# A four-layer trunk on one core: the program's head loads its vectors from another queue and re-orders its first steps

## The chip, the cores and the metric

The kernel runs on one core of one Trainium2 chip. The metric is the device time of one execution in microseconds (us), on the slowest core, which here is the only one.

## The reference

The reference puts 16 meta tokens ahead of 512 tokens of 1024 channels (528 tokens in all) and runs four layers. Each layer is a mixer and a gated feed-forward block, each added to the residual `h`. The mixers are pooling (layers 0 and 3), differential attention (layer 1) and a conformer convolution (layer 2). All is in fp32. Only the start of layer 0 matters here:

```python
h = jnp.concatenate([meta, x], axis=1)
y = rmsnorm(h, norm_mix_g[0])                   # over 1024 channels
# pool_mixer: per group of 256 channels, windows 2, 4, 8, 16
pooled = stack([trailing_mean(y_g, win) - y_g for y_g, win in groups])
mixed = einsum('blgc,gcd->blgd', pooled, pool_w[0]).reshape(B, L, 1024)
h = h + (mixed + pool_b[0]) * pool_scale[0]
h = h + swiglu_ffn(rmsnorm(h, norm_ffn_g[0]), ...)   # then layers 1 to 3
```

## The kernel before

Channels lie on the 128 partitions in 8 blocks, tokens along the free dimension. Every product of fp32 matrices is made of three rounded ones: each operand is split into a high half (`_hi`, a rounding copy on ScalarE) and a low half (`_lo`, a subtraction on VectorE), and TensorE adds hi\*hi, hi\*lo and lo\*hi. The program is written engine by engine; semaphores order the engines, and each engine runs its list in order.

The head of the program is all that the change touches. Before layer 0 can begin:

- SyncE (SP) issues six loads of `x` into `x_rows` (five tiles of tokens: 128, 128, 128, 127 and 32 rows; L639 to L643). It then waits until GpSimd has zeroed `vec_rows` (L779) and issues twelve loads of small vectors into `vec_rows`, 50 rows of 1024 floats (L649 to L654: norm gains, biases, convolution taps). Then come the four tiles of pool weights (`w_raw`, L659), the lambda vectors, and the bias table.
- TensorE runs 6 fill matmuls whose result nobody reads (`unread`, L1716), transposes the five tiles of `x_rows` (L1725), 6 more fills, waits for all twelve vector loads, transposes `vec_rows` (L1731), 15 fills, then begins the pool products `z` (L1039: 120 matmuls on `y` and the pool weights).
- VectorE copies each transposed tile into `h` (L3021), then the vectors into `vec` (L3027), which raises `vec_ready`.
- ScalarE sums the squares of the rows of each tile of x (L2199, the token sums), splits two pool weight tiles (L1802), waits for `vec_ready`, and makes the eight blocks `y_hi` (L1807) with two more weight halves between. It then rounds the band matrices (`bands`, L1856), the small matrices that take the trailing means.

After that VectorE turns the token sums into row factors (L2426 and the steps behind it, `tok_ready`), but only behind the low part of `bands` (L2478). ScalarE scales `z` by them into `z_hi` (L1874, five tiles, two `add_bias` steps L1862 between), VectorE makes `z_lo` (L2495), and TensorE multiplies z by the bands (`windows`, L1078 to L1087). The first of these waits for four tiles of `z_lo`. From there on TensorE works through windows, feed-forward and the later layers.

Of the kernel before, what the change touches and what calls it, by code (L numbers as in the profile page):

```python
# [31 lines left out]
ACT = mybir.ActivationFunctionType  # L32
ds = bass.ds

P = 128
# [5 lines left out]
NB = D // P  # L41
# [7 lines left out]
TAPS = 31  # L49
# [10 lines left out]
TILES = 5  # L60
# [293 lines left out]
class Semaphores:  # L354

    def __init__(self, sem):
# [5 lines left out]
        self.bias_in = sem("bias_in")  # L363
        self.gain_in = sem("gain_in")
        self.out_done = sem("out_done")
        self.vec_zeroed = sem("vec_zeroed")
        self.vec_ready = sem("vec_ready")
        self.consts_ready = sem("consts_ready")
        self.rel_ready = sem("rel_ready")
# [200 lines left out]
def trunk(nc, a, out):  # L570
    cols, first = plan()
    tiles = len(cols)
    ctx = ExitStack()
    with ctx:
# [62 lines left out]
        def _(sp):  # L637
# [3 lines left out]
            for i in range(1, TILES):  # L641
                t, n = TILE_STARTS[i] - META, LAST if i == TILES - 1 else P
                sp.dma_start(m.x_rows[0:n, i, :], a["x"][0, t:t + n, :]).then_inc(x_in[i], 16)  # L643
            sp.wait_ge(s.vec_zeroed, 1)
            for row, name in ((ROW_MIX, "norm_mix_g"), (ROW_FFN, "norm_ffn_g"), (ROW_POOL_B, "pool_b"),
                              (ROW_POOL_S, "pool_scale"), (ROW_DWB, "conv_dw_b"), (ROW_LNG, "conv_ln_g"),
                              (ROW_LNB, "conv_ln_b"), (ROW_CONV_OUT, "conv_b_out")):
                n = a[name].shape[0]
                sp.dma_start(m.vec_rows[row:row + n, :], a[name]).then_inc(s.vec_in, 16)  # L649
            sp.dma_start(m.vec_rows[ROW_CONV_IN:ROW_CONV_IN + 2, :],  # L650
                         a["conv_b_in"].rearrange("o (r n) -> (o r) n", r=2)).then_inc(s.vec_in, 16)
            for t, n in ((0, 16), (16, TAPS - 16)):
                sp.dma_start(m.vec_rows[ROW_DW + t:ROW_DW + t + n, :], a["conv_dw_w"][0, t:t + n, :]).then_inc(s.vec_in, 16)
            sp.dma_start(m.vec_rows[ROW_SUBLN:ROW_SUBLN + 1, 0:P], a["attn_subln_g"]).then_inc(s.vec_in, 16)  # L654

            def load(off, i, per, src, at_col, width):

                slot = off % SLOTS
# [117 lines left out]
        @block.gpsimd  # L776
        def _(pool):

            pool.memset(m.vec_rows[:, :], 0.0).then_inc(s.vec_zeroed, 1)  # L779
            pool.memset(m.tok_x[:, :], 1.0).then_inc(s.tok_cleared, 1)  # L780
            pool.memset(m.rms_eps, RMS_EPS)
            pool.memset(m.ln_eps, LN_EPS)
# [188 lines left out]
        def _(pe):  # L971
# [741 lines left out]
            def unread(n):  # L1713

                for _ in range(n):
                    pe.matmul(ps[:, 6, 0:P], m.ones[:, :], m.ones[:, :], start=True, stop=True)  # L1716
# [3 lines left out]
            for i, n in enumerate(TILE_ROWS):  # L1720
# [4 lines left out]
                    mm = pe.transpose(ps[:, 2 * (i % 3) + d // 4, (d % 4) * P:(d % 4) * P + n],  # L1725
                                      m.x_rows[0:n, i, d * P:(d + 1) * P], m.ident[0:n, 0:n])
                mm.then_inc(s.rows_turned, 1)
            unread(6)
            pe.wait_ge(s.vec_in, 16 * 12)
            for d in range(NB):  # L1730
                mm = pe.transpose(ps[:, 7, d * ROWS:(d + 1) * ROWS], m.vec_rows[:, d * P:(d + 1) * P],  # L1731
# [61 lines left out]
        def _(act):  # L1793
            def split_hi(t, i, per, n):

                if n == 0:
                    return
                slot = t % SLOTS
                act.wait_ge(raw_in[slot], (i * (per // SLOTS) + (t // SLOTS + 1 + pairs_done(first, t))) * 16)
                if t >= SLOTS:  # L1800
                    act.wait_ge(s.tile_used, i * per + (t - SLOTS + 1))
                act.activation(m.w_hi[:, slot, 0:n], m.w_raw[:, slot, 0:n], ACT.Copy).then_inc(s.hi_ready, 1)  # L1802

            def y_hi(d, hn, yn, row, t0, n):

                act.wait_ge(s.h_ready, d + (NB * hn + 1))
                act.activation(blk(m.y_hi, d, t0, n), blk(m.h, d, t0, n), ACT.Copy, scale=vec_col(row, d))\  # L1807
                   .then_inc(s.y_hi_ready, 1)
# [38 lines left out]
            def pool_layer(name, which, r, y_in, hn, yn, row):  # L1847
                tile0 = first[name]
                if name == "pool0":
                    act.wait_ge(s.vec_ready, 1)  # L1850
                    for d in range(NB):
                        y_hi(d, H_IN, Y_POOL0, ROW_MIX + 0, 0, TOK)
                        if d in (1, 3):
                            split_hi(tile0 + (3 + d) // 2, 0, 0, cols[tile0 + (3 + d) // 2])
                    act.wait_ge(s.band_built, 1)
                    act.activation(m.bands[:, :, 0:LOW0], m.bands_raw[:, :, :], ACT.Copy).then_inc(s.band_hi_ready, 1)  # L1856
                else:
                    act.wait_ge(s.token_sums, r + 1)
                act.wait_ge(s.vec_bias_ready, 1)
                def add_bias(d):  # L1860
                    act.wait_ge(s.y_ready, NB * y_in + d + 1)
                    act.activation(blk(m.h, d), blk(m.h, d), ACT.Identity, bias=m.pool_bs[:, which, d:d + 1])\  # L1862
                       .then_inc(s.h_biased, 1)
                if name == "pool0":
                    act.wait_ge(s.band_ready, 1)
                    act.dma_start(bands_dram, m.bands[:, :, :].bitcast(F32)).then_inc(s.bands_out, 16)
                act.wait_ge(s.tok_ready, which + 1)
                for i in range(TILES):
                    if i < TILES - 1:
                        act.wait_ge(s.z_done, (TILES - 1) * which + i + 1)  # L1870
                    else:
                        act.wait_ge(s.tile_used, tile0 + 4)
                    base, n = 2 * (i % 4), TILE_ROWS[i]
                    act.activation(m.z_hi[0:n, i, :].rearrange("p (b n) -> p b n", b=2), ps[0:n, base:base + 2, :],  # L1874
                                   ACT.Copy, scale=m.tok_r[0:n, i:i + 1]).then_inc(s.z_hi_ready, 1)
                    if i in (1, 2) and name == "pool0":
                        add_bias(i - 1)
                for c in (4, 5):
                    split_hi(tile0 + c, 0, 0, cols[tile0 + c])
                if name == "pool0":  # L1880
                    add_bias(2)
                for d in range(NB):
                    y_hi(d, hn, yn, row, 0, TOK)
                    act.activation(blk(m.x_square, d), blk(m.h, d), ACT.Square).then_inc(s.square_ready, 1)
                    if name == "pool0" and d + 3 < NB:
                        add_bias(d + 3)
                if name == "pool0":
                    act.wait_ge(s.rel_ready, 1)
                    act.dma_start(rel_once, m.rel[:, :]).then_inc(s.rel_once_out, 16)
# [303 lines left out]
                        split_hi(first["attn_out"] + NB + c, 0, 0, 512)  # L2193

            act.wait_ge(s.tok_cleared, 1)
            for i, n in enumerate(TILE_ROWS):
                act.wait_ge(x_in[i], 32 if i == 0 else 16)
                e = act.activation(m.row_squares[0:n, i, :], m.x_rows[0:n, i, :], ACT.Square,  # L2199
                                   accum_out=m.tok_x[0:n, i:i + 1])  # L2200
            e.then_inc(s.token_sums, 1)
            for t in range(2):
                split_hi(t, 0, 0, cols[t])
            pool_layer("pool0", 0, R_POOL0, Y_POOL0, H_POOL0, Y_FFN0, ROW_FFN + 0)
            act.wait_ge(s.lam_sums, 1)
            act.activation(m.lam_s[:, 2:4], m.lam_s[:, 0:2], ACT.Exp).then_inc(s.lam_exps, 1)
# [146 lines left out]
        def _(dve):  # L2353
            def split_lo(t, i, per, n):

                if n == 0:
                    return
                slot = t % SLOTS
                dve.wait_ge(s.hi_ready, i * per + (t + 1))
                dve.tensor_tensor(m.w_lo[:, slot, 0:n], m.w_raw[:, slot, 0:n],  # L2360
                                  m.w_hi[:, slot, 0:n].bitcast(F32), ALU.subtract).then_inc(s.lo_ready, 1)

            def y_lo(d, yn, row, t0, n):

                dve.wait_ge(s.y_hi_ready, d + (NB * yn + 1))
                dve.scalar_tensor_tensor(out=blk(m.y_lo, d, t0, n), in0=blk(m.h, d, t0, n), scalar=vec_col(row, d),
                                         in1=blk(m.y_hi, d, t0, n).bitcast(F32), op0=ALU.mult, op1=ALU.subtract)\
                   .then_inc(s.y_ready, 1)
# [89 lines left out]
            def pool_layer(name, which, r, yn, hn, row):  # L2458
# [9 lines left out]
                                             in1=blk(m.h, d), op0=ALU.mult, op1=ALU.add).then_inc(s.h_ready, 1)  # L2468

                if name == "pool0":  # L2470
                    for c in (0, 1):
                        split_lo(tile0 + c, 0, 0, cols[tile0 + c])
                    for d in range(NB):
                        y_lo(d, Y_POOL0, ROW_MIX + 0, 0, TOK)
                        if d in (1, 3):
                            split_lo(tile0 + (3 + d) // 2, 0, 0, cols[tile0 + (3 + d) // 2])
                    dve.wait_ge(s.band_hi_ready, 1)
                    dve.tensor_tensor(m.bands[:, :, LOW0:BANDS], m.bands_raw[:, :, FIRST0:FIRST0 + EDGE],  # L2478
                                      m.bands[:, :, FIRST0:FIRST0 + EDGE].bitcast(F32), ALU.subtract)\
                       .then_inc(s.band_ready, 1)  # L2480
# [544 lines left out]
            e.then_inc(s.h_ready, NB)  # L3025
            dve.wait_ge(s.rows_turned, TILES + 1)
            dve.tensor_copy(m.vec[:, :], ps[:, 7, 0:NB * ROWS]).then_inc(s.vec_ready, 1)  # L3027
            dve.drain()
            by_block = m.vec[:, :].rearrange("p (d r) -> p r d", d=NB)
            dve.tensor_tensor(m.pool_bs[:, :, :], by_block[:, ROW_POOL_B:ROW_POOL_B + 2, :],  # L3030
                              by_block[:, ROW_POOL_S:ROW_POOL_S + 2, :], ALU.mult).then_inc(s.vec_bias_ready, 1)
# [242 lines left out]
```

## Time and profile before

| | us |
|---|---|
| median of 3 runs | 1983.63 (1983.15 to 1984.39) |
| the profiled execution | 1983.36 |
| its span in the trace | 1981.6 |
| TensorE busy | 1965.5 (99%) |
| VectorE busy | 1569.5 (79%) |
| ScalarE busy | 933.8 (47%) |
| GpSimd busy | 208.6 (11%) |
| mean DMA rate | 99 GB/s |

Times in rows are microseconds from the span's start unless marked ns. PE is TensorE (PEld its weight loads), DVE VectorE, ACT ScalarE, POOL GpSimd, SP SyncE; a q behind an engine's name is its sequencer, where DMAs are issued. A busy TensorE is not always useful: fills count as busy too. An fp32 matmul on `ones` shows as two records, so 15 fills are 30 records.

### The profile page before, as it was taken

What the parts mean: (1) busy time and instruction counts of PE and PEld (TensorE: products, weight loads), DVE (VectorE), ACT (ScalarE), POOL (GpSimd) and SP (SyncE); (2) the same over time, 40 slices, a digit from 0 to 9 for tenths busy, and PEclk for the clock granted to TensorE, in tenths of its full rate; (3) what the DMA queues carried; (4) which work ended last, traced back from release to release, by engine and by line L of the source; (5) the groups of instructions that cost most, each with busy time, mean ns of one, the idle gap of its engine ahead of it and who ended that gap; (6) DMA issues with size and microseconds to landing.
All of it is one profiled execution on the core that took longest, in us unless ns stands there. A gap on an engine that the chain in (4) does not pass through costs nothing.

```text
span 1981.6 us, 39851 instructions
## 1 busy us (share of the span) xinstructions
PE 1965.5 (99%) x15718; PEld 1909.9 (96%) x15718; DVE 1569.5 (79%) x2171; ACT 933.8 (47%) x1484; POOL 208.6 (11%) x325
## 2 busy tenths in 40 slices
PE   9999999999999999999999999999999999999998
PEld 8999999999999999999999989999999998989997
DVE  6797788767788788877979997697778768977794
ACT  7443333346676534433447785343334454433343
POOL 5000000241111200000051212000000140000000
PEclk9999999999999999999999999999999999999999
DMA  5433342342111324233335762223243323323232
GB/s 171 140 86 106 86 127 81 92 129 64 54 57 52 96 86 128 67 103 93 94 113 130 163 139 64 86 86 107 85 126 85 114 70 107 112 80 104 86 107 96
DMA packets 305390, 196.82 MB, mean 99 GB/s; under 512 B 7450, under 2 KB 297243, under 8 KB 305012
## 3 DMA queue, kind: packets, MB, share of 16 engines
q1 hardware_dynamic: 298972, 175.08, 30.8%
q0 software_dynamic: 5104, 15.71, 3.8%
q10 hardware_dynamic: 1192, 4.34, 0.6%
q8 instruction: 84, 1.38, 0.3%
q14 instruction: 38, 0.31, 0.1%
HBM read 179.45 MB, written 6.44 MB: 94 GB/s over the span
## 4 chain that ended last, share of the span: by engine, by line
PE 88%; DVE 5%; issue 3%; ACT 2%; DMA 1%; DVEq 1%; SPq 0%; POOLq 0%; ACTq 0%
PE ps L977 43%; PE ps L1276 35%; PE ps L1387 2%; PE ps L1039 1%; PE ps L1232 1%; DVE cv_odd L3133 1%; PE ps L1459 1%; DVE cv L3133 1%; PE ps L1087 1%; PE ps L1500 1%; DMA cv_sum<-cv 1%; PE ps L1488 0%; PE ps L1512 0%; DVE w_lo L2604 0%; DVEq L2640 0%
## 5 line engine op out<-in xcount | busy, mean ns | idle before, releaser
L1276 PE MATMUL ps<-t_lo,y_hi 128*128 128x264 f32 (+1 forms) x1008 | 285.7, 283 | 0.0
L1276 PE MATMUL ps<-t_lo,w_hi 128*128 128x264 f32 (+1 forms) x1008 | 285.7, 283 | 0.0
L1276 PE MATMUL ps<-t_hi,w_lo 128*128 128x264 f32 (+1 forms) x1008 | 285.4, 283 | 0.0
L1276 PE MATMUL ps<-t_hi,y_lo 128*128 128x264 f32 (+1 forms) x1008 | 285.3, 283 | 0.0
L1276 PE MATMUL ps<-t_hi,w_hi 128*128 128x264 f32 (+1 forms) x1008 | 285.0, 283 | 0.0
L1276 PE MATMUL ps<-t_hi,y_hi 128*128 128x264 f32 (+1 forms) x1008 | 284.8, 283 | 0.0
L1934 ACT ACTIVATE w_hi<-w_raw 128x1024 fp32r<-128x1024 f32 (+1 forms) x108 | 127.8, 1201 | 330.1 <-PE ps L977 193.9
L977 PE MATMUL ps<-hid_hi,w_hi 128*128 128x264 f32 (+1 forms) x1184 | 265.4, 296 | 1.6 <-DVE hid_lo L2660 1.5
L977 PE MATMUL ps<-hid_lo,w_hi 128*128 128x264 f32 (+1 forms) x1184 | 264.6, 296 | 0.0
L977 PE MATMUL ps<-hid_hi,w_lo 128*128 128x264 f32 (+1 forms) x1184 | 264.2, 296 | 0.0
L977 PE MATMUL ps<-y_hi,w_hi 128*128 128x264 f32 (+1 forms) x1088 | 240.6, 297 | 0.7 <-issue 0.3
L977 PE MATMUL ps<-y_lo,w_hi 128*128 128x264 f32 (+1 forms) x1088 | 233.6, 291 | 0.0
L977 PE MATMUL ps<-y_hi,w_lo 128*128 128x264 f32 (+1 forms) x1088 | 233.5, 291 | 0.0
L1934 ACT ACTIVATE y_hi<-w_raw 128x1024 fp32r<-128x1024 f32 (+1 forms) x108 | 125.8, 1196 | 166.5 <-DVE w_raw L2614 133.5
L977 PEld LDWEIGHTS ps<-hid_hi,w_hi 128*128 128x128 f32 x1184 | 187.2, 188 | 7.9 <-DVE hid_lo L2660 1.9
L977 PEld LDWEIGHTS ps<-hid_lo,w_hi 128*128 128x128 f32 x1184 | 187.7, 188 | 5.5
L977 PEld LDWEIGHTS ps<-hid_hi,w_lo 128*128 128x128 f32 x1184 | 187.4, 188 | 5.6
L1276 PEld LDWEIGHTS ps<-t_hi,w_hi 128*128 128x128 f32 x1008 | 189.8, 188 | 0.3 <-DVE h L2700 0.2
L1276 PEld LDWEIGHTS ps<-t_hi,y_hi 128*128 128x128 f32 x1008 | 189.8, 188 | 0.0
L1276 PEld LDWEIGHTS ps<-t_lo,w_hi 128*128 128x128 f32 x1008 | 189.5, 188 | 0.1
L1276 PEld LDWEIGHTS ps<-t_hi,w_lo 128*128 128x128 f32 x1008 | 189.5, 188 | 0.0
L1276 PEld LDWEIGHTS ps<-t_hi,y_lo 128*128 128x128 f32 x1008 | 189.5, 188 | 0.0
(410 smaller groups left out, 4333.8 us busy)
## 6 DMA issues: line engine op xcount, KB each, us to landing
w_raw<-in_ffn_w_gate SPq DMA_DIRECT2D x88, 512.0 KB, 5.1
w_raw<-in_ffn_w_up SPq DMA_DIRECT2D x88, 512.0 KB, 4.8
w_raw<-in_ffn_w_down SPq DMA_DIRECT2D x70, 512.0 KB, 4.4
w_raw<-in_ffn_w_down SPq DMA_DIRECT2D x24, 384.0 KB, 4.3
w_raw<-in_attn_w_qkv SPq DMA_DIRECT2D x16, 512.0 KB, 3.7
w_raw<-in_conv_w_in SPq DMA_DIRECT2D x16, 512.0 KB, 4.1
w_lo<-w_raw POOLq DMA_DIRECT2D x16, 512.0 KB, 5.1
w_raw<-in_attn_w_qkv SPq DMA_DIRECT2D x16, 256.0 KB, 2.9
```

The costliest lines, as they stand in the source:

```text
L977: mm = pe.matmul(ps[:, bank + hf, 0:half], w[:, slot, col:col + P], x(hf), start=begin and w is m.w_hi and n == 0, stop=end and w is m.w_lo)
L1039: mm = pe.matmul(out, y[:, at:at + rows], w[:, (t0 + g) % SLOTS, k * 256:(k + 1) * 256], start=k == 0 and n == 0, stop=k == 1 and n == 2)
L1087: mm = pe.matmul(out[:, c0:c1], z, m.bands[0:TILE_ROWS[i], g, at:at + c1 - c0], start=i == 2 and n == 0, stop=i in (1, 4) and n == 1)
L1232: mm = pe.matmul(ps[:, 2 * g + hf, 0:HALF], w[:, (tile0 + g) % SLOTS, k * P:(k + 1) * P], x[:, at:at + HALF], start=k == 0 and n == 0, sto ...
L1276: mm = pe.matmul(ps[:, bank, 0:hw], w[:, at:at + P], b[:, t, k, 0:hw], start=k == 0 and n == 0, stop=k == 3 and n == 2)
L1387: mm = pe.matmul(bank, x, w, start=False, stop=k == LAST_F - 1 and n == 2)
L1459: mm = pe.matmul(ps[:, (4, proj_banks(par, 1))[part] + c, col:col + k1 - k0], q[rows, 0, q0:q0 + P], k[rows, 1, k0:k1], start=n == 0, stop ...
L1500: mm = pe.matmul(ps[:, 4, i * P:QT * P], v, w, start=False, stop=i == QT - 1 and x == 2)
L1934: act.activation(hi[:, sub * SUB:(sub + n_sub) * SUB], src, ACT.Copy).then_inc(s.op_hi, 1)
L3133: dve.scalar_tensor_tensor(out=sums[n % 2], in0=u, scalar=vec_col(ROW_DW + tap, c), in1=sums[n % 2], op0=ALU.mult, op1=ALU.add).then_inc(s ...
```

## The change

- The twelve vector loads are issued by ScalarE at the program's start, with no zeroing of `vec_rows` and no wait. `attn_subln_g` (128 floats) is written eight times, so that its whole row is filled.
- SP therefore issues the pool weights right behind x.
- TensorE's six fills between the transposes of x and those of the vectors are gone.
- ScalarE no longer sums the squares of the fifth tile of x with the others, but behind the last `y_hi`, and weight halves and `y` halves alternate, both on ScalarE and on VectorE.
- VectorE waits for its own semaphore instead of draining before `pool_bs`.

```diff
@@ SyncE
-            sp.wait_ge(s.vec_zeroed, 1)
-            for row, name in ((ROW_MIX, "norm_mix_g"), (ROW_FFN, "norm_ffn_g"), ...
-                sp.dma_start(m.vec_rows[row:row + n, :], a[name]).then_inc(s.vec_in, 16)
...
-            sp.dma_start(m.vec_rows[ROW_SUBLN:ROW_SUBLN + 1, 0:P], a["attn_subln_g"]).then_inc(s.vec_in, 16)
@@ GpSimd
-            pool.memset(m.vec_rows[:, :], 0.0).then_inc(s.vec_zeroed, 1)
@@ TensorE
-            unread(6)
             pe.wait_ge(s.vec_in, 16 * 12)
@@ ScalarE, pool_layer
-                    act.wait_ge(s.vec_ready, 1)
                     for d in range(NB):
+                        if d % 2 == 0:
+                            split_hi(tile0 + d // 2, 0, 0, cols[tile0 + d // 2])
+                        if d == 0:
+                            act.wait_ge(s.vec_ready, 1)
                         y_hi(d, H_IN, Y_POOL0, ROW_MIX + 0, 0, TOK)
-                        if d in (1, 3):
-                            split_hi(tile0 + (3 + d) // 2, 0, 0, cols[tile0 + (3 + d) // 2])
+                    row_squares(TILES - 1).then_inc(s.token_sums, 1)
                     act.wait_ge(s.band_built, 1)
@@ ScalarE, head
+            for row, name in ((ROW_MIX, "norm_mix_g"), (ROW_FFN, "norm_ffn_g"), ...
+                act.dma_start(m.vec_rows[row:row + n, :], a[name]).then_inc(s.vec_in, 16)
...
+            act.dma_start(m.vec_rows[ROW_SUBLN:ROW_SUBLN + 1, :].rearrange("p (d c) -> p d c", d=NB),
+                          bass.AP(a["attn_subln_g"].tensor, 0, [[P, 1], [0, NB], [1, P]])).then_inc(s.vec_in, 16)
             act.wait_ge(s.tok_cleared, 1)
-            for i, n in enumerate(TILE_ROWS):
+            def row_squares(i):
...
-            for t in range(2):
-                split_hi(t, 0, 0, cols[t])
+            for i in range(TILES - 1):
+                row_squares(i)
@@ VectorE, pool_layer
-                    for c in (0, 1):
-                        split_lo(tile0 + c, 0, 0, cols[tile0 + c])
                     for d in range(NB):
+                        if d % 2 == 0:
+                            split_lo(tile0 + d // 2, 0, 0, cols[tile0 + d // 2])
                         y_lo(d, Y_POOL0, ROW_MIX + 0, 0, TOK)
-                        if d in (1, 3):
-                            split_lo(tile0 + (3 + d) // 2, 0, 0, cols[tile0 + (3 + d) // 2])
@@ VectorE, head
-            dve.drain()
+            dve.wait_ge(s.vec_ready, 1)
```

ScalarE from its first row squares to the bands, before (the square of the 32-row tile stands third):

```order
L2199 ACTIVATE row_squares,tok_x<-x_rows 128x1024 x3
L2199 ACTIVATE row_squares,tok_x<-x_rows 127x1024
L2199 ACTIVATE row_squares,tok_x<-x_rows 32x1024
L1802 ACTIVATE w_hi<-w_raw 128x512 x2
L1807 ACTIVATE y_hi<-h,vec 128x528 x2
L1802 ACTIVATE w_hi<-w_raw 128x512
L1807 ACTIVATE y_hi<-h,vec 128x528 x2
L1802 ACTIVATE w_hi<-w_raw 128x512
L1807 ACTIVATE y_hi<-h,vec 128x528 x4
L1856 ACTIVATE bands<-bands_raw 128x4x783
```

and the same stretch of ScalarE now (the line numbers are those of the changed kernel: L2200 squares, L1787 weight halves, L1792 `y_hi`, L1843 bands):

```order
L2200 ACTIVATE row_squares,tok_x<-x_rows 128x1024 x3
L2200 ACTIVATE row_squares,tok_x<-x_rows 127x1024
L1787 ACTIVATE w_hi<-w_raw 128x512
L1792 ACTIVATE y_hi<-h,vec 128x528 x2
L1787 ACTIVATE w_hi<-w_raw 128x512
L1792 ACTIVATE y_hi<-h,vec 128x528 x2
L1787 ACTIVATE w_hi<-w_raw 128x512
L1792 ACTIVATE y_hi<-h,vec 128x528 x2
L1787 ACTIVATE w_hi<-w_raw 128x512
L1792 ACTIVATE y_hi<-h,vec 128x528 x2
L2200 ACTIVATE row_squares,tok_x<-x_rows 32x1024
L1843 ACTIVATE bands<-bands_raw 128x4x783
```

Between the first `y_hi`, which waits for the vectors, and the bands there stand now three weight halves instead of two, and one square of rows that stood ahead of them.

TensorE from the transposes of x to the first pool product, before:

```order
L1725 MATMUL ps<-ident,x_rows 128x128 x24
L1725 MATMUL ps<-ident,x_rows 128x127 x8
L1725 MATMUL ps<-ident,x_rows 128x32 x8
L1716 MATMUL ps<-ones 128x128 x6
L1731 MATMUL ps<-ident,vec_rows 128x50 x8
L1716 MATMUL ps<-ones 128x128 x15
L1039 MATMUL ps<-w_hi,y_hi 128x256
```

and now (L1711 transposes x, L1716 the vectors, L1702 fills, L1025 pool products):

```order
L1711 MATMUL ps<-ident,x_rows 128x128 x24
L1711 MATMUL ps<-ident,x_rows 128x127 x8
L1711 MATMUL ps<-ident,x_rows 128x32 x8
L1716 MATMUL ps<-ident,vec_rows 128x50 x8
L1702 MATMUL ps<-ones 128x128 x15
L1025 MATMUL ps<-w_hi,y_hi 128x256
```

The six fills ahead of the vectors' transposes are gone; the fifteen behind them stay.

## Rows read from the trace of the kernel before

**Rows 1.** The page: busy time by engine, and the chain by engine

```profile
PE 1965.5 (99%) x15718; PEld 1909.9 (96%) x15718; DVE 1569.5 (79%) x2171; ACT 933.8 (47%) x1484; POOL 208.6 (11%) x325
PE 88%; DVE 5%; issue 3%; ACT 2%; DMA 1%; DVEq 1%; SPq 0%; POOLq 0%; ACTq 0%
```

**Rows 2.** Chain of waits, 0 to 62 us: start, duration, what

```profile
7.25 5.69 DMA vec_rows<-in_attn_subln_g
...
13.68 3.54 PE ps L1716 x30
...
17.27 14.46 PE ps L1039 x120
31.73 0.73 PE ps L1127 x6
...
32.50 0.38 PE ps L1078
...
59.04 3.07 PE ps L977 x23
```

**Rows 3.** Waits, 0 to 59.5 us: in total, times, longest

```profile
PEld ps L1078 <- DVE z_lo L2495: 0.3, 1, 0.3
```

**Rows 4.** Timeline of VectorE: start, duration, instruction, [idle before it and what ended it]

```profile
6.85 5.22 DVE L3021 COPY h<-ps 128x512 f32<-128x512 f32 x10 [6.85 <-PE ps L1725]
...
13.71 0.57 DVE L3027 COPY vec<-ps 128x400 f32<-128x400 f32 x1 [1.64 <-PE ps L1731]
...
31.16 1.28 DVE L2495 SCALAR_TENSOR_TENSOR z_lo<-ps,tok_r,z_hi 127x1024 fp32r<-127x1024 f32 x1 [0.35 <-ACT z_hi L1874]
```

**Rows 5.** Timeline of ScalarE, 5 to 34 us

```profile
5.17 1.28 ACT L2199 ACT_TABLE_LOAD   x1 [5.17 <-DMA x_rows<-in_x]
...
10.64 1.04 ACT L2199 ACTIVATE row_squares<-x_rows 32x1024 f32<-32x1024 f32 x1
...
13.18 1.38 ACT L1802 ACTIVATE w_hi<-w_raw 128x512 fp32r<-128x512 f32 x2 [1.40 <-DMA w_raw<-in_pool_w]
14.46 1.35 ACT L1807 ACTIVATE y_hi<-h,vec 128x528 fp32r<-128x528 f32 x2
15.71 0.61 ACT L1802 ACTIVATE w_hi<-w_raw 128x512 fp32r<-128x512 f32 x1
...
20.51 2.81 ACT L1856 ACTIVATE bands<-bands_raw 128x3132 fp32r<-128x3132 f32 x1
...
25.75 2.12 ACT L1874 ACTIVATE z_hi<-ps,tok_r 128x1024 fp32r<-128x1024 f32 x2 [2.43 <-DVEq L2429]
...
31.77 1.11 ACT L1874 ACTIVATE z_hi<-ps,tok_r 32x1024 fp32r<-32x1024 f32 x1 [0.64 <-PE ps L1039]
```

**Rows 6.** Timeline of TensorE's weight loads, 5 to 14 us

```profile
10.29 0.57 PEld L1725 LDWEIGHTS ps<-ident,x_rows 32*128 32x128 f32 x8 [0.17 <-DMA x_rows<-in_x]
...
12.98 0.57 PEld L1731 LDWEIGHTS ps<-ident,vec_rows 50*128 50x128 f32 x8 [0.66 <-DMA vec_rows<-in_attn_subln_g]
```

**Rows 7.** Windows: length, busy PE, PEld, DVE, ACT, POOL, PEclk, DMA share, GB/s

```profile
2.50:3.50 1.00, 0.72 (x3) 0.72 (x4) 0.00 (x0) 0.00 (x0) 1.00 (x2) 1.00 0.85 225
3.50:5.00 1.50, 1.50 (x9) 1.50 (x8) 0.00 (x0) 0.00 (x0) 1.50 (x1) 1.00 1.04 344
5.00:8.50 3.50, 3.47 (x27) 3.24 (x26) 1.65 (x3) 3.31 (x5) 3.13 (x36) 1.00 1.04 408
```

**Rows 8.** Windows of the fills alone (L1716): length, busy PE, PEld, PEclk, DMA

```profile
2.50:5.50 3.00, 2.72 (x12) 2.63 (x12) 1.00 0.97 313
...
13.60:17.24 3.64, 3.62 (x30) 3.42 (x30) 1.00 0.31 70
```

**Rows 9.** Timeline of TensorE around its longest later idle time for ScalarE

```profile
1167.49 0.39 PE L1106 MATMUL ps<-u_hi,tap_hi 64*128 64x264 f32 x2 [1.19 <-ACT tap_lo L2270]
```

**Rows 10.** Timeline, DMA issues and GpSimd's zeroing at the head

```profile
0.81 0.94 POOL L779 MEMSET vec_rows<- 50x1024 f32 x1 [0.29 <-POOLq L3265]
...
55.81 0.76 ACTq L2209 DMA_DIRECT2D rel_scratch<-rel_once  x1
```

More of the change, by code:

```diff
@@ L365, in __init__ @@
         self.out_done = sem("out_done")
-        self.vec_zeroed = sem("vec_zeroed")
         self.vec_ready = sem("vec_ready")
@@ L643, in _ @@
                 sp.dma_start(m.x_rows[0:n, i, :], a["x"][0, t:t + n, :]).then_inc(x_in[i], 16)
-            sp.wait_ge(s.vec_zeroed, 1)
[L645 to L648, printed above, removed]
-                sp.dma_start(m.vec_rows[row:row + n, :], a[name]).then_inc(s.vec_in, 16)
[L650 to L653, printed above, removed]
-            sp.dma_start(m.vec_rows[ROW_SUBLN:ROW_SUBLN + 1, 0:P], a["attn_subln_g"]).then_inc(s.vec_in, 16)
             def load(off, i, per, src, at_col, width):
@@ L2193, in attention_step @@
                         split_hi(first["attn_out"] + NB + c, 0, 0, 512)
+            for row, name in ((ROW_MIX, "norm_mix_g"), (ROW_FFN, "norm_ffn_g"), (ROW_POOL_B, "pool_b"),
+                              (ROW_POOL_S, "pool_scale"), (ROW_DWB, "conv_dw_b"), (ROW_LNG, "conv_ln_g"),
+                              (ROW_LNB, "conv_ln_b"), (ROW_CONV_OUT, "conv_b_out")):
+                n = a[name].shape[0]
+                act.dma_start(m.vec_rows[row:row + n, :], a[name]).then_inc(s.vec_in, 16)
+            act.dma_start(m.vec_rows[ROW_CONV_IN:ROW_CONV_IN + 2, :],
+                         a["conv_b_in"].rearrange("o (r n) -> (o r) n", r=2)).then_inc(s.vec_in, 16)
+            for t, n in ((0, 16), (16, TAPS - 16)):
+                act.dma_start(m.vec_rows[ROW_DW + t:ROW_DW + t + n, :], a["conv_dw_w"][0, t:t + n, :]).then_inc(s.vec_in, 16)
+            act.dma_start(m.vec_rows[ROW_SUBLN:ROW_SUBLN + 1, :].rearrange("p (d c) -> p d c", d=NB),
+                          bass.AP(a["attn_subln_g"].tensor, 0, [[P, 1], [0, NB], [1, P]])).then_inc(s.vec_in, 16)
             act.wait_ge(s.tok_cleared, 1)
-            for i, n in enumerate(TILE_ROWS):
+            def row_squares(i):
+                n = TILE_ROWS[i]
                 act.wait_ge(x_in[i], 32 if i == 0 else 16)
-                e = act.activation(m.row_squares[0:n, i, :], m.x_rows[0:n, i, :], ACT.Square,
-                                   accum_out=m.tok_x[0:n, i:i + 1])
-            e.then_inc(s.token_sums, 1)
-            for t in range(2):
-                split_hi(t, 0, 0, cols[t])
+                return act.activation(m.row_squares[0:n, i, :], m.x_rows[0:n, i, :], ACT.Square,
+                                      accum_out=m.tok_x[0:n, i:i + 1])
+            for i in range(TILES - 1):
+                row_squares(i)
             pool_layer("pool0", 0, R_POOL0, Y_POOL0, H_POOL0, Y_FFN0, ROW_FFN + 0)
```

## The prediction, made before the changed kernel ran

> **What bounds the kernel now.** I read the page first. TensorE is busy for 99% of the span and makes 88% of the chain [rows 1], and nothing behind the head is changed. So the change can only move the moment at which TensorE's unbroken work begins. Next I read the chain of waits from 0 to 62 us. TensorE waits for the last vector load (landed at about 12.94), makes 15 fills, begins the pool products at 17.27, ends them at 31.73, makes six fills and begins the windows at 32.50 [rows 2]. By this view everything before 17.27 is in series with the end, and what the head gives is won.
>
> The waits tell more. At 32.50 TensorE was not the last to be ready: its weight loads had idled 0.3 us for the low half of z [rows 3], of which the fourth piece ended at 31.16 + 1.28 = 32.44 [rows 4]. So a second chain ends within 0.3 us of the first, and the chain view shows only one of them. ScalarE's timeline gives it: `y_hi` from 14.46, bands from 20.51, then `z_hi` from 25.75, after 2.43 us of waiting for the row factors [rows 5], which VectorE computes only behind the bands. The bands begin when ScalarE is through with its list, so work put ahead of them there moves the windows one for one: 32.50 - 20.51 = 11.99 us from bands to windows. I call V the start of the copy of the vectors, 13.71 before [rows 4]. ScalarE's first `y_hi` starts 14.46 - 13.71 = 0.75 behind V. From the first windows on TensorE is in series to its next block at 59.04 [rows 2], so what moves 32.50 moves the end.
>
> **The change, part by part.** The sum is for the windows' start.
>
> 1. ScalarE between V and the bands. Before, 20.51 - 14.46 = 6.05 us for eight `y_hi` and two weight halves. Now three halves stand there: + 0.61. The fifth square of rows stands there too: + 1.04 [rows 5]. Where they stood they cost nothing, because ScalarE waited 1.40 us before 13.18 for the pool weights [rows 5]. Bands now begin at V + 0.75 + 6.05 + 0.61 + 1.04 = V + 8.45, where it was V + 6.80, and the windows at V + 8.45 + 11.99 = V + 20.44. That is a loss of 1.65 us against V.
>
> 2. V itself. The vectors are no longer late. V is then set by two other things. VectorE copies h without a pause from 6.85 to 12.07 [rows 4]: V is not before 12.07. And TensorE had the last tile of x at 10.29; its transposes take 0.57 and those of the vectors, to V, 13.71 - 12.98 = 0.73 [rows 4, 6]: V = 11.59 + D, if the last tile of x comes D later than before. With D = 0 the gain in V is 1.64 us and the windows begin at 12.07 + 20.44 = 32.51: nothing is won.
>
> 3. D, the delay of x. The vector loads now run beside x instead of behind it. The DMA engines are full: share 1.04 at 408 GB/s from 5.00 to 8.50 us [rows 7]. Bounds: D = 0, if the vectors find gaps, and D = 12.98 - 10.29 = 2.69 us, all that lay between the release of the last tile of x and that of the vectors [rows 6], if the vectors all go first. Part of this is already in the 10.29: the three windows of [rows 7] move 0.225 + 0.516 + 1.428 = 2.17 MB by 8.50, and x is 544 rows of 4096 bytes, 2.23 MB, so x had nearly all moved 1.8 us before its last tile released TensorE. I take off 0.5 and use D = 1.4, about the middle: V = 12.99 and the windows begin at 33.43, **0.93 us later than before**. The bounds give 32.51 (+0.01) and, with V = 14.28, 34.72 (+2.22).
>
> The rows show full DMA engines, and no stretch in which two queues compete. The Trainium skill ("DMA: Bandwidth & Descriptors", Queues, rings and completion order) says that each DMA engine takes turns between the queues that have work for it. By that rule the vectors get a turn beside every packet of x on the engines they use, and D is near its upper half. The same page (Issuing engines are not separate DMA queues) says that issuing from a second engine saves only issue time, which speaks against this part of the change; without competition the sum would be +0.01.
>
> 4. TensorE's own line. The 15 fills behind the vectors' transposes stay, so pool products begin at V + 17.27 - 13.71 = V + 3.56 = 16.55, 0.72 us sooner. Of this nothing arrives: they end at V + 18.02 and the six fills behind them at V + 18.79, when the windows wait until V + 20.44. A new wait of 1.65 us on the low half of z takes the place of the old wait on the vectors.
>
> 5. At nothing: twelve issues on ScalarE, at 0.76 each (its costliest issue near the head [rows 10]) done by 10 us, at half of that by 5.4, about when x's first tile arrives at 5.17 [rows 5]. Four squares, the table load and one half, 6.1 us in all, then have to be done by V + 0.75 = 13.7, so 2 us are to spare in the likely case, and in the worst the first `y_hi` would be late by about 2. The zeroing, 0.94 us [rows 10], only brings the first fills forward. Pool weights released ScalarE at 13.18 [rows 5] and move up four issues; they are needed at V. The fifth `z_hi` no longer waits for TensorE (0.64 [rows 5]), but the windows begin without it. VectorE's halves alternate as ScalarE's do and hide behind them. The wait for its own semaphore costs what the drain did.
>
> The sum: +0.93, of 1983.36 in the profiled execution (1981.6 of span and 1.8 around it), 1984.3. The runs' median, 1983.63, lies 0.27 above that execution, so I give 1984.6.
>
> **Rivals.**
>
> A. No competition: x lands as before, D = 0, and the windows begin at 32.51. The time is the old one, 1983.6. For it: vector loads are 200 KB, 0.5 us at the full rate. Against it: 2.69 us lay between the last tile of x and the vectors.
>
> B. What the chain view promises: the pool products begin sooner and all of it arrives. With D = 0 they begin at 15.63, which is 1.64 us sooner, 1982.0. This needs the bands to be off the path. Against it: the 0.3 us in [rows 3] leaves at most 0.3 of room.
>
> C. Slower by much: TensorE's clock. The first fills are busy for 2.72 us with 12 records where the fifteen later ones take 3.62 for 30, 0.23 against 0.12 us each [rows 8], though the PEclk column prints 1.00 for both: these are 1.2 and 2.4 GHz. Six fills are gone, and gaps in the transposes grow as x comes late. If all fifteen fills run at the lower level they take 6.9 instead of 3.6 us. Pool products then begin at V + 6.9, the windows at V + 6.9 + 14.46 + 0.77 = V + 22.1: with V = 12.99 that is 35.1, +2.6 us, 1986.2. It decides once the fills are more than 1.65 us longer than now, that is with about half of them at the lower level. The new pause of 1.65 us before the windows adds risk: the longest late wait for ScalarE on record is 1.19 us, after which the clock was still full [rows 9]. With the upper bound of D as well the loss is 3.9 us.
>
> **How the numbers follow.** The forecast (windows 0.3 to 2.2 us later, by the bands and by late x) has 0.62, rival A 0.17, B 0.06, C 0.11, and 0.04 are left for what I did not see. The time is that of the forecast, 1984.6. The forecast's bounds alone give 1983.6 to 1985.9. The range goes on below by the runs' own scatter (0.5 below their median) and reaches into C: 1983.1 to 1986.6. A measurement of this kernel can tell about 0.2%, 4.0 us, from no change. Only C with a late V passes that on the slow side, 0.04; the whole wait on the vectors is less than that on the fast side, 0.01.
>
> **What would show it.** Right: in the new trace V near 13.0, the pool products sooner than 17.27, bands starting 8.4 us behind V, a wait of 1 to 2 us of TensorE on the low half of z before the first window, the first window later than 32.50, and everything behind it as before. D shows in the wait for the last tile of x (10.29 before). Rival A: that tile at 10.3 and a first window at 32.5. B: no wait on z. C: records of the fifteen fills of 0.24 us. I am wrong if the first window begins before 32.2, or if something behind 59.04 moves by another amount than the windows do.

## The result: 0.25% slower, and the head loses more than it should

| | before | changed |
|---|---|---|
| median | 1983.39 us (10 runs, 1982.47 to 1987.60) | 1988.53 us (10 runs, 1986.94 to 1991.91) |
| ratio, 95% interval | | 1.0025 [1.0017, 1.0033] |
| profiled execution, its span | 1983.36, 1981.6 | 1989.90, 1988.2 |
| vectors' copy (V) | 13.71 | 17.31 |
| pool products begin | 17.27 | 23.06 |
| first window | 32.50 | 37.95 |

The forecast was 1984.6 in a range of 1983.1 to 1986.6: wrong, too low by 3.9 us and outside the range. The first window is 5.45 us later, not 0.93. Chain of waits after (start, duration, what), answering [rows 2]:

```profile
2.67 10.59 DMA x_rows<-in_x
...
13.30 2.94 PE ps L1711 x16
16.25 1.02 PE ps L1716 x8
17.27 6.03 PE ps L1702 x30
23.30 14.08 PE ps L1025 x120
37.38 0.73 PE ps L1113 x6
38.11 0.23 PE ps L1064
```

(A piece of the chain starts where the piece before it ends, so some starts read up to 0.3 us later than the instruction's own in the table.) The vectors have left the chain and x has taken their place. The fifteen fills take 6.03 us, before 3.54. Weight loads of TensorE after, with the wait before them in brackets, answering [rows 6]:

```profile
11.47 0.91 PEld L1711 LDWEIGHTS ps<-ident,x_rows 128*128 128x128 f32 x8 [2.47 <-DMA x_rows<-in_x]
13.30 1.56 PEld L1711 LDWEIGHTS ps<-ident,x_rows 127*128 127x128 f32 x8 [0.92 <-DMA x_rows<-in_x]
15.19 0.92 PEld L1711 LDWEIGHTS ps<-ident,x_rows 32*128 32x128 f32 x8 [0.33 <-issue]
16.18 0.93 PEld L1716 LDWEIGHTS ps<-ident,vec_rows 50*128 50x128 f32 x8
```

The fourth tile of x (127 rows) comes at 13.30. Before, the same row read:

```profile
9.27 0.85 PEld L1725 LDWEIGHTS ps<-ident,x_rows 127*128 127x128 f32 x8 [0.71 <-DMA x_rows<-in_x]
```

That is 4.03 us later, and the same eight transposes take 1.56 instead of 0.85. Windows after (length, busy PE, PEclk, DMA share, GB/s) show the second fact:

```profile
10.00:12.00 2.00, 0.52 (x5) 1.00 1.06 220
12.00:14.00 2.00, 1.48 (x10) 0.55 1.11 341
14.00:17.00 3.00, 3.00 (x22) 0.50 0.32 63
17.00:20.00 3.00, 3.00 (x16) 0.50 0.00 0
20.00:22.00 2.00, 2.00 (x11) 0.50 0.79 231
22.00:24.00 2.00, 2.00 (x18) 0.89 0.84 236
24.00:38.00 14.00, 14.00 (x122) 1.00 0.58 202
```

TensorE was busy for 0.52 of 2 us while it waited for x; then the granted clock was 0.50 (1.2 GHz) through the last transposes and most of the fills (the clock records of the trace have the fall at 12.21 and the rise at 22.45). VectorE and ScalarE after, answering [rows 4, 5]:

```profile
17.31 0.57 DVE L3026 COPY vec<-ps 128x400 f32<-128x400 f32 x1 [0.34 <-PE ps L1716]
...
36.62 1.28 DVE L2494 SCALAR_TENSOR_TENSOR z_lo<-ps,tok_r,z_hi 127x1024 fp32r<-127x1024 f32 x1 [0.35 <-ACT z_hi L1861]
```

```profile
17.91 1.36 ACT L1792 ACTIVATE y_hi<-h,vec 128x528 fp32r<-128x528 f32 x2 [2.88 <-DVE vec L3026]
...
24.50 1.04 ACT L2200 ACTIVATE row_squares<-x_rows 32x1024 f32<-32x1024 f32 x1
...
25.54 2.80 ACT L1843 ACTIVATE bands<-bands_raw 128x3132 fp32r<-128x3132 f32 x1
```

The bands begin at V + 8.23, where I had worked out V + 8.45. The low half of z ends at 37.90, 0.05 before the first window, while TensorE is only just through with the pool products: the two chains end together. And the DMA windows, answering [rows 7]:

```profile
2.50:3.50 1.00, 1.00 (x6) 1.00 (x6) 0.00 (x0) 0.00 (x0) 1.00 (x1) 1.00 0.52 152
3.50:5.00 1.50, 1.32 (x7) 1.02 (x5) 0.00 (x0) 0.00 (x0) 1.38 (x4) 1.00 1.04 311
5.00:8.50 3.50, 1.44 (x11) 1.20 (x12) 0.68 (x2) 1.77 (x2) 3.21 (x34) 1.00 1.04 368
```

0.152 + 0.467 + 1.288 = 1.91 MB had moved by 8.50, vectors included, where it had been 2.17 MB of x nearly alone. With the engines just as full (1.04), less arrives. The packet records of the traces count x itself: before, all its 544 rows had moved by 8.67 us; now 472 had moved by 9.00, and the last one was through at 13.05.

### The profile page after: what moved, and what is told of

Same layout as the page of the kernel before. It is cut to its first block, busy times and chain, and to the rows that moved or that the text cites. A ratio compares the mean times of both kernels' runs of the same rounds, so it can differ in the third digit from the quotient of the medians.

```text
span 1988.2 us, 39825 instructions
## 1 busy us (share of the span) xinstructions
PE 1968.2 (99%) x15706; PEld 1912.0 (96%) x15706; DVE 1570.3 (79%) x2171; ACT 933.6 (47%) x1484; POOL 210.3 (11%) x324
## 4 chain that ended last, share of the span: by engine, by line
PE 87%; DVE 5%; issue 3%; ACT 2%; DVEq 1%; DMA 1%; POOL 0%; POOLq 0%; SPq 0%; ACTq 0%
PE ps L963 44%; PE ps L1262 33%; PE ps L1092 2%; PE ps L1373 2%; PE ps L1025 1%; PE ps L1218 1%; PE ps L1073 1%; DVE w_lo L2603 1%; PE ps L1486 1%; PE ps L1445 1%; DVEq L2639 1%; DVEq L2608 1%; DMA x_rows<-in_x 1%; DMA w_raw<-in_ffn_w_down 1%; DVE y_lo L2603 0%
```

## The experiments

Theory T1: late x, from vector loads beside it, and the low clock that follows from the wait; plus 1.65 us for the new order on ScalarE. T2: the order is the main loss. T3: the six missing fills made the clock fall. All shifts below are of one profiled execution each, against V 13.71, bands 20.51, first window 32.50. "Tile 4" is the release of the 127-row tile of x (9.27 before). Where TensorE itself was behind, I give the landing of that tile's load (9.23 before).

**e1, the loads alone** (the kernel before, with the `dma_start` of the vectors moved to ScalarE's start and no `vec_zeroed`; SP's pool weights so move up right behind x, issued from 3.72 us instead of 7.54):

```diff
-            sp.wait_ge(s.vec_zeroed, 1)
-                sp.dma_start(m.vec_rows[row:row + n, :], a[name])
+                act.dma_start(m.vec_rows[row:row + n, :], a[name])
```

> The kernel before with one part of the change: ScalarE issues the twelve vector loads at once, nothing is zeroed, pool weights follow x. The order of halves and squares and the six fills stay as before. Theory 1 (the vectors take turns with x on the engine that carries all of them, so x is late): the last tile of x releases TensorE near 13.3 (10.3 before), V (start of the copy of the vectors) 16.3 to 17.3, first window between V + 18.8 = 35 and, if the clock is low for the fifteen fills, 38; time +3 to +5 us. Theory 2 (the order of ScalarE's list is what costs, the loads cost nothing): last tile of x at 10.3, first window 32.5 or sooner, time 0 or -1.

Measured: 1988.64 against 1983.69, ratio 1.0021 [1.0012, 1.0030]. Tile 4 at 12.47, V 19.30, first window 39.14. The row is

```profile
12.47 1.52 PEld L1712 LDWEIGHTS ps<-ident,x_rows 127*128 127x128 f32 x8 [2.39 <-DMA x_rows<-in_x]
```

The low clock is there (1.52 for the eight) with all fills in place; the eight weight loads of the tile before took 0.14 us each, which is the full clock, so here too it fell behind the wait. V and the first window came later than the ranges I had given (16.3 to 17.3, 35 to 38). So the moved loads, without the new order, make a loss as large as the whole. Whether x is late by the vectors beside it or by the weights behind it, e1 does not separate (see step 3 below).

**e2, the order alone** (the kernel before, with halves alternating and the fifth square last, as in the change's two `pool_layer` pieces).

> The kernel before with another part: ScalarE and VectorE alternate weight halves and y halves, the fifth square stands behind the last y_hi. The loads, the zeroing and all fills stay. Theory 1 and my working of the bands' chain: V stays 13.7, bands begin at V + 8.4 = 22.1 (20.5 before), first window at 34.1, time +1.6 us, with TensorE waiting 1.6 us on the low half of z. Theory 2 (order is all of it): first window at 36 or later, +4 us or more. Rival (order is nothing): 32.5, 0.

Measured: 1984.52 against 1983.69, ratio 1.0005 [0.9996, 1.0014]. V 14.07, bands 22.32 (V + 8.25), first window 34.31 (V + 20.24), clock full. Step 1 stands by itself: 1.45 us against V (20.24, before 18.79); the other 0.36 of the 1.81 us in the head is V, with x landing later. In the time, 0.8 us, it is not clear of noise. T2, which wanted 36 or later here, is out. TensorE waits as foretold, here weight loads in total, times, longest:

```profile
PEld ps L1078 <- DVE z_lo L2497: 0.8, 1, 0.8
```

**e3, the six fills back** in the changed kernel:

```diff
                 mm.then_inc(s.rows_turned, 1)
+            unread(6)
             pe.wait_ge(s.vec_in, 16 * 12)
```

> The changed kernel with the six fills put back between the transposes of x and those of the vectors. Theory 3 (TensorE's clock fell because the six fills are gone): no stretch at the lower clock, fifteen fills in 3.6 us, pool products near 20; first window then waits for z near 37.2, time -0.9 against the changed kernel. Theory 1 (the clock fell because TensorE waited for x, ahead of the place of the six fills): the lower clock still holds from about 12 us on, the six fills take 3 us at it, and the first window comes at the same time or up to 3 us later than 38.1.

Measured: 1990.76 against 1983.69, ratio 1.0031 [1.0019, 1.0043]; first window 40.41. The fills ran at the lower level (12 records in 2.86 us, where e2's chain has 1.53) and pushed V on to 19.75. But in this execution the clock did not fall behind the wait for x. It had never risen, from the first tile of x on, though six fills had run from 1.90 to 4.5 us (the trace records the rise at 24.14):

```profile
5.81 1.57 PEld L1711 LDWEIGHTS ps<-ident,x_rows 128*128 128x128 f32 x8 [1.28 <-DMA x_rows<-in_x]
```

So putting the six fills back does not save the head, and at that place they cost 2.5 us of it (40.41 against 37.95). That their absence never lowers the clock does not follow; see e4.

**e4, the vectors behind x** (the changed kernel with all twelve loads on SP behind x, not waiting for zeroing):

```diff
-                act.dma_start(m.vec_rows[row:row + n, :], a[name])
+                sp.dma_start(m.vec_rows[row:row + n, :], a[name])
```

> The changed kernel, but SP issues the twelve vector loads behind x and ahead of the pool weights, as before though without zeroing. Theory 1: x as before, last tile at 10.3, V 13.7, first window at V + 20.4 = 34.1, which is 4 us sooner than in the changed kernel; time +1.6 against the kernel before. Theory 3 (the missing fills alone lower the clock): V 13.7 to 14, fifteen fills in 6 us, pool products at 19.8, first window near 35; +2.5. Theory 2: first window stays near 38, +5.

Measured: 1986.70 against 1983.69, ratio 1.0017 [1.0008, 1.0026]. V 14.19, first window 34.48 (V + 20.29).

```profile
5.46 6.03 PEld L1723 LDWEIGHTS ps<-ident,x_rows 128*128 128x128 f32 x32 [0.94 <-DMA x_rows<-in_x]
13.46 0.57 PEld L1728 LDWEIGHTS ps<-ident,vec_rows 50*128 50x128 f32 x8 [1.23 <-DMA vec_rows<-in_attn_subln_g]
```

Tile 4 landed at 9.93, much as in e2 (10.13) and e8 (9.95): x is on time. (That TensorE never waits for x after 5.46 says less, since it turned most of these 32 blocks at the lower level.) What is left of the loss in the head is the order's 1.50 us and 0.48 of V. The clock fell here too, with x on time, behind the 1.23 us that TensorE waited for the vectors. The fifteen fills took 5.24 us instead of 3.62:

```profile
14.08 5.05 PEld L1714 LDWEIGHTS ps<-ones 128*128 128x128 f32 x30
14.00:17.50 3.50, 3.50 (x19) 0.52 0.23 47
```

The pool products began at 19.09 = V + 4.90, where T3 had said 19.8. It cost the head nothing, for the windows waited for the low half of z until 34.42. So T3 is out as the cause of late x and of the loss, but not as a way to the low clock: with six fills in that place, as in e2, there was no wait for the vectors and the clock stayed full.

**e5, only the two tall loads beside x** (`conv_dw_w`, 124 of the 200 KB, on ScalarE; ten small ones on SP behind x; else the changed kernel).

> The changed kernel, but only the two conv_dw_w loads (16 and 15 rows, 124 of the 200 KB) are issued by ScalarE at once; the ten loads of 1 to 4 rows are issued by SP behind x and ahead of the pool weights. Theory 1 (the loads of few rows land on one and the same DMA engine, and the number of loads is what delays x): the last tile of x releases TensorE at 10.3 to 11.0, V 13.3 to 14.2, first window 33.8 to 34.7, time +1.5 to +3 against the kernel before. Rival (bytes delay x, so 62% of them give 62% of the delay): last tile of x at 12.1 or later, first window 35.5 or later.

Measured: 1987.29 against 1984.36, ratio 1.0014 [1.0005, 1.0023]. V 14.20, first window 34.47, tile 4 landed at 9.82. So 62% of the bytes cost next to nothing there. Most of the delay comes with the ten small loads, 76 KB, or with the pool weights, which stand behind those ten here (from 7.67 us) and right behind x in the changed kernel.

**e6, fills while x is late** (the changed kernel):

```diff
-            unread(6)
+            unread(9)
             for i, n in enumerate(TILE_ROWS):
+                if i in (2, 3):
+                    unread(6)
```

> The changed kernel with TensorE kept busy while it waits for x: nine fills at the start instead of six, and six fills each ahead of the third and the fourth tile of x. The loads are those of the changed kernel. Theory (of the 5.6 us, about 3.3 are the late x and the rest the lower clock): fills and transposes run at the full clock from some 6 us on, V near 14.8 (17.3 in the changed kernel), fifteen fills in 3.6 us, first window at V + 20.4 = 35.2, time 2.5 to 3 us under the changed kernel. Rival (the clock falls whatever is put between, or the fills cost as much as they give): lower clock seen again between 12 and 22 us, first window at 37.5 or later.

Measured: 1989.46 against 1984.36, ratio 1.0031 [1.0018, 1.0043]. In the head as T1 wants: tile 4 no sooner (12.28), clock full, V 15.00, first window 35.23, 2.7 us sooner than in the changed kernel's first profile. Its second (e9) has 35.28 without these fills, so the gain in the head is not shown beyond scatter. The time does not follow either: my 2.5 to 3 us less was a miss (see e9, e10).

**e7, the small loads from GpSimd** (the kernel before without zeroing, nine small loads issued by GpSimd, the rest by ScalarE, pool weights right behind x, eight first fills).

> The kernel before, without the zeroing: GpSimd issues the nine loads of 1 to 4 rows behind the identity matrix, ScalarE the two conv_dw_w loads and the sub-norm gain at the start, SP the pool weights right behind x; eight first fills instead of six; order of halves and squares as before. Theory 1 with a queue that spreads one-row loads over 16 engines (the built program shows them as 1x16x64): last tile of x at 10.3 to 10.8, V 12.1 to 12.8, first window at V + 18.8 = 30.9 to 31.6, time -0.9 to -1.6 us. Rival (GpSimd's issues are dear, about 1 us each, so the band matrices, ready at 14.1 before and needed at V + 6.8, come at 22 or later): first window at 34 or later, +1.5 us.

Measured: 1990.02 against 1984.36, ratio 1.0035 [1.0021, 1.0049]. Tile 4 at 11.61, V 15.51, first window 38.55. I had expected x on time (its last tile at 10.3 to 10.8, it was 12.63) and V at 12.1 to 12.8, since this queue spreads a one-row load (64 packets of 256 bytes for four of them): a miss that speaks against the few engines as the whole reason. A new wait took over:

```profile
26.52 2.83 ACT L1852 ACTIVATE bands<-bands_raw 128x3132 fp32r<-128x3132 f32 x1 [4.24 <-POOL bands_raw L808]
```

GpSimd builds the band matrices, and its issues stand ahead of that.

**e8, row factors first** (the kernel before; VectorE makes the row factors ahead of the low part of the bands and alternates its halves, 12 fills instead of 15).

> The kernel before, with its loads as they were: VectorE computes the row factors ahead of the low part of the bands instead of behind it, alternates weight halves and y halves (ScalarE does not), and twelve fills stand where fifteen did. Theory (two chains end together at the first window, that of TensorE and that over the bands): both are shortened, pool products at V + 2.9 = 16.6, z_hi from 24.5 on, the first window bound by TensorE at V + 18.1 = 31.8, time -0.7 us. Rival (the bands' chain does not pass the row factors): first window stays at 32.4 behind z, 0.

Measured: 1984.17 against 1984.36, ratio 1.0001 [0.9992, 1.0010]. V 14.10, first window 32.86 = V + 18.76, as before (V + 18.79). The row factors no longer held `z_hi`, but the pool products did: nothing won, where I had expected 0.7 us.

**e9, the changed kernel again, e10, late x alone, e11, a try at beating both,** in the same runs. e10 is e6 with halves and fifth square in their old order. e11 is e5 with that old order and `unread(9)` first.

> The changed kernel again, beside the next two and the kernel before in the same runs, to size the whole against its head. My theory (late x, the low clock that follows, and the bands 1.65 us later against V): the first window near 38.1 us, where it was 32.50, and the time 5 to 6 us over the kernel before. Rival (part of the loss lies behind the head, in the attention layer): the time more than 7 us over, or the stretch between the first feed-forward product and the end more than 1 us longer than before in this execution too.

> The changed kernel with 9 first fills and 6 more ahead of each of tiles 3 and 4 of x (so that TensorE is never idle for long while it waits for x), and with the halves and the fifth square back in their order before. What is left of the change is the vectors' loads from ScalarE beside x. My theory: V near 15.0, bands 6.8 behind V at 21.8, the first window at V + 18.8 = 33.8, clock full: 1.3 us later than before, and the time about 4 us less than the changed kernel's in the same runs. Rival (the fills only move the head and the time doesn't follow): the head like this, but the time within 1 us of the changed kernel's.

> A try at beating both: the two tall loads (31 rows) from ScalarE at once, the ten small ones from SP right behind x without waiting for zeroing, 9 first fills, no fills between, and the halves and squares in their order before. My theory: x as before (last tile at 10.3 to 11), V 13.0 to 13.7 by the ten issues on SP, the first window at V + 18.8 = 31.8 to 32.5: no gain to 0.7 us of gain, too small to tell in the time. Rival (V is set by how late the ten loads land behind x, 14.2 as with six first fills): first window near 33.0, 0.5 later than before.

Measured, against 1983.53: e9 1988.04, ratio 1.0020 [1.0011, 1.0029]; e10 1987.49, 1.0023 [1.0014, 1.0032]; e11 1984.86, 1.0006 [0.9997, 1.0015]. The first windows are at 35.28, 33.94 and 32.14 (e11's V 13.49). Weight loads of the fourth tile in e9, e10 and e11:

```profile
12.34 0.85 PEld L1711 LDWEIGHTS ps<-ident,x_rows 127*128 127x128 f32 x8 [2.53 <-DMA x_rows<-in_x]
```

```profile
12.55 0.85 PEld L1713 LDWEIGHTS ps<-ident,x_rows 127*128 127x128 f32 x8 [0.30 <-DMA x_rows<-in_x]
```

```profile
10.78 0.85 PEld L1721 LDWEIGHTS ps<-ident,x_rows 127*128 127x128 f32 x8 [1.05 <-DMA x_rows<-in_x]
```

The same kernel, in e9's execution, had its x 1 us sooner than at first, and the clock fell later and for less time (from 14.38 to 17.80):

```profile
10.00:12.00 2.00, 0.05 (x1) 1.00 1.09 251
12.00:14.00 2.00, 1.66 (x17) 1.00 1.08 321
14.00:16.00 2.00, 2.00 (x15) 0.60 0.27 51
16.00:18.00 2.00, 2.00 (x12) 0.55 0.04 9
18.00:20.00 2.00, 2.00 (x21) 1.00 0.86 256
```

V was 15.06 and the first window 35.28, 20.22 behind it, 2.78 later than before: my expectation, near 38.1, was a miss. In that execution the clock cost nothing, because the pool products (19.54) had room behind the wait for z, and 2.78 us is late x plus the order. So the head's loss is not one number.

For the rest of the program I lined up the start of every TensorE instruction with the same one before; shift in us (median of 8 us of instructions) by the place in the kernel before:

```
place       60    150    430    700   1000   1700    end
changed   5.37   5.22   5.52   6.66   6.59   6.38   6.54
e9        2.71   2.75   2.89   3.60   3.55   3.57   4.61
e1        6.56   6.59   6.58   6.87   6.84   7.51   6.60
e2        1.79   1.64   1.64   4.20   4.20   4.51   4.55
e10       1.37   1.37   3.00   3.82   5.18   5.22   4.13
e6        2.64   2.68   3.87   4.20   5.44   5.38   4.92
e8        0.35   0.38   0.38   0.40   0.40   0.16   0.91
e11      -0.37  -0.36  -0.36  -0.18  -0.24   0.13   0.07
```

The head's shift travels unchanged for 90 us. Then there are steps of 0.3 to 2.6 us at a few places. One sits at 441 us: e2 stands there, and VectorE was late for TensorE behind GpSimd's wait for a DMA.

```profile
444.79 0.19 PEld L1459 LDWEIGHTS ps<-qk_hi 64*128 64x128 f32 x2 [1.95 <-DVE k L2898]
```

Two others, near 164 and 787 us, are in e6 and e10 alone, where the first block's down weights came late; in e10:

```profile
167.21 0.30 PEld L963 LDWEIGHTS ps<-hid_hi,w_hi 128*128 128x128 f32 x2 [1.61 <-DVE hid_lo L2659]
```

These two steps, 1.6 and 1.4 us in e10, are why its head gained 1.34 us on e9's and its median only 0.55: the rival I had set against e10 came true. Both kernels hold 36 fills, the others 21 to 29; why the weights then come late I can't say. e11 did best in the head, 0.37 us sooner at 60 us, but its median is not below the kernel before's. No version beat it.

## Why the prediction was wrong, by its own steps

1. ScalarE between V and bands: right. V + 8.23 to V + 8.25 measured (V + 8.45 worked out), windows at V + 20.2 to V + 20.3 in e2, e4 and e9 (V + 20.44). This part alone costs 1.45 us against V (e2), where I had 1.65.

2. V = 11.59 + D: nearly right. From the release of tile 4 to V there are 2.72 us in both e9 and e10, where my terms give 11.59 - 9.27 = 2.32. I took VectorE's copies of h as a fixed bound (12.07), but they too wait for tile 4: in e10 the last four take 1.67 us from 13.67 and V follows at 15.27, with TensorE's transposes out of the way. That is 0.40 us more.

3. D: this is the step that failed. I used 1.4, with 2.69 as upper bound. By the release of tile 4 it was 3.07 (e9) and 4.03 us (first profile) in the changed kernel, and 3.28 in e10. Executions that left the loads alone had tile 4 at 10.17 (e2) and 9.99 (e8), so 0.7 to 0.9 of it may be scatter. The bound was read from where the vectors landed behind x. That says what they take when x is through, not what they take from x.
One rival is only half settled. In each execution with x late the pool weights were issued right behind x, from 3.6 to 3.8 us; in each with x on time from 7.5 us or later. In the first profile their first packet began at 9.76 us, and by 9.00 x was already 72 rows behind (472 of 544, where all had moved before): that part is not theirs. What they add to the last rows no run separates; e1 with the weights held back would.

The sum of the first profile: V was 17.31 where I had 12.99. Of these 4.32 us, 2.63 are D (4.03 for 1.4), 0.40 are VectorE's copies, and 1.29 are the lower clock in front of V, which no term of mine had.

4. TensorE's own line: pool products were to begin at V + 3.56. They began at V + 5.75 in the first profile (23.06) and at V + 4.48 in e9 (19.54), not sooner than before but later; with the clock full it was V + 3.25 (e6).

Rival C, to which I gave 0.11, happened in its clock but not by its price. The fills ran at the lower level and the pool products began at V + 5.75 (V + 6.9 foretold); that brought them level with the wait for z, not past it. What the clock cost was in front of V, where I had not looked: the transposes took 4.01 us from tile 4 to V instead of 2.72. So 5.45 = 1.29 of slow transposes + 2.31 of late x (the rest of V's 3.60, the vectors' old wait already paid out of it) + 1.43 of order (8.23 - 6.80) + 0.42 between bands and window (12.41, before 11.99). In e1, with the old order, C's mechanism decided: TensorE came last, 39.14 = V + 19.84, past the V + 18.79 that z allows, though short of the V + 22.1 of all fills at the lower level. I named the cause of C as the missing fills and the gaps together. The executions fit the gaps: the clock fell behind a wait of 2.4 to 2.5 us for x in the first profile, e1 and e9, and stayed full in e6 and e10, where work was put into that wait. They do not give a rule: e7 kept it with waits of 1.40 and 1.59 us for x, e4 lost it behind 1.23 us for the vectors, which the missing fills had left open, e5 kept it behind 0.73, and in e3 it never rose. That is one execution of each, two of the changed kernel. I should have tied C to D, since late x brings such waits.

Rivals A and B are out: x did come later, and no gain of the vectors arrived. "Everything behind as before" was wrong too: in the first profile 6.54 - 5.37 = 1.2 us was added behind the head, of a kind that e2 has as well. These steps differ between executions, so they move spans. The medians of all runs (+5.1, e9 +4.5) are nearer to the first profile's head (5.45) than to e9's (2.78); how much of them is the head and how much lies behind it, two profiles do not settle.

## What to carry to other kernels

A load that is issued sooner takes its turns from whatever is loading then: move it only if what it runs beside is not what the first engine waits for. Look at how few engines the small ones can use, and at what moves up in the queue that they leave. When the critical load gets later, price with it the lower TensorE clock that its wait may leave behind, and hold useful or idle matmuls for the wait itself rather than behind it; here that kept the clock (e6, e10) but did not pay in the time. Before taking a wait away, read the second chain that ends beside it: here it was 0.3 us off and the new order made it 1.45 us longer.

## What was not expected of the hardware

- After a stretch with TensorE busy for 0.05 of 2 us (e9) the granted clock was still 1.00 over the next 2 us, with TensorE busy again for 1.66 of them, and 0.60 over the 2 us after that. The fall shows behind the idle time, so it is paid by what follows.
- In e3 the PEclk column prints 1.00 from the start although the transposes' eight weight loads took 1.57 us for each of the first three tiles and 1.56 for the fourth, as at 1.2 GHz (0.85 at 2.4). The trace's first clock record is the rise, at 24.14, and the column is 1.00 ahead of it; a column of ones at the head is no proof of the full clock, the durations are:

```profile
12.89 1.56 PEld L1711 LDWEIGHTS ps<-ident,x_rows 127*128 127x128 f32 x8 [0.77 <-DMA x_rows<-in_x]
```

```profile
12.00:14.00 2.00, 1.63 (x8) 1.00 1.11 337
```

- Two executions of one kernel differ by 2.7 us in the first window (37.95 and 35.28): one profile sizes a head to a few us only.
